# Half of the first tile's output projection summed inside the attention steps of three mixers

## What is computed

```python
def ab_mixer(x, ...):
    ...
    return jnp.concatenate([y_a, y_b], axis=-1) @ w_o

def nsa_mixer(x, ...):
    ...
    return o.reshape(B, S, C_MIX) @ w_o

def _gqa_attention(...):
    ...
    y_lat = jnp.moveaxis(o, 0, 1).reshape(b, n, Q_DIM) @ w_o
```

## Time and profile before

| what | value |
|---|---|
| median of 3 runs | 1934.36 us (1932.5 to 1934.42) |
| the profiled execution, its own time | 1922.37 us |
| its span | 1920.6 us |
| mean granted TensorE clock | 0.92 of full speed |
| PE busy | 1538.6 us (80%) |
| DVE busy | 424.4 us (22%) |
| ACT busy | 248.4 us (13%) |
| moved by DMA | 711.11 MB, mean 370 GB/s |

### The profile page before, as it was taken

The page is one execution under the profiler, slowest core; times in us unless marked ns, Lnnn a source line. Parts: engine busy times, 40 slices in busy tenths (PEclk is TensorE's granted clock), DMA queues, the critical chain, the costliest instruction groups (busy, mean ns, idle before and its releaser), DMA issues.

```text
span 1920.6 us, 23284 instructions
## 1 busy us (share of the span) xinstructions
PE 1538.6 (80%) x10228; PEld 742.0 (39%) x10228; DVE 424.4 (22%) x944; ACT 248.4 (13%) x531; POOL 86.7 (5%) x142
## 2 busy tenths in 40 slices
PE   7898777899898788999977667776799767667676
PEld 4665434664464344444522122221355222122222
DVE  3341110226331112464500000000043000000001
ACT  0310000026312011155100000000011000000000
POOL 1100000101100000112100000000000000000000
PEclk9999899999999999999998888887999888888888
DMA  7559999859879999299599999999987999999996
GB/s 286 216 226 415 423 423 421 313 206 386 338 304 409 420 421 416 92 366 394 224 425 423 424 424 423 423 424 424 420 333 313 423 424 424 423 423 423 424 423 269
DMA packets 128014, 711.11 MB, mean 370 GB/s; under 512 B 8376, under 2 KB 13480, under 8 KB 59296
## 3 DMA queue, kind: packets, MB, share of 16 engines
q1 hardware_dynamic: 121488, 697.14, 88.8%
q0 software_dynamic: 4320, 9.78, 1.5%
q10 hardware_dynamic: 2096, 2.57, 0.4%
HBM read 708.17 MB, written 1.05 MB: 369 GB/s over the span
## 4 chain that ended last, share of the span: by engine, by line
PE 46%; DMA 42%; DVE 5%; SPq 2%; ACT 2%; issue 2%; POOL 1%; DVEq 0%; PEldq 0%; ACTq 0%; POOLq 0%
DMA ring<-in_moe_w 23%; DMA ring<-in_moe_w_down 6%; PE pa L812 6%; PE pb L785 5%; DMA work<-in_moe_w 5%; PE pa L830 4%; PE pb L762 3%; DMA mod<-in_moe_w 3%; PE acc L883 3%; PE acc L1382 3%; PE acc L1387 3%; PE acc L1123 2%; SPq L698 2%; DMA ring<-in_moe_w_up 2%; DMA work<-in_moe_w_down 2%
## 5 line engine op out<-in xcount | busy, mean ns | idle before, releaser
L785 PE MATMUL pb<-ring,XT 128*32 128x512 f32 x1424 | 274.2, 716 | 90.8 <-DMA ring<-in_moe_w 90.5
L812 PE MATMUL pa<-ring,work 128*32 128x512 f32 x928 | 188.2, 742 | 68.8 <-DMA ring<-in_moe_w 44.5
L785 PEld LDWEIGHTS pb<-ring,XT 128*32 128x32 f32 x1424 | 62.3, 127 | 252.8 <-DMA ring<-in_moe_w 131.6
L929 DVE TENSOR_TENSOR work<-work,pb 128x256 f32<-128x256 f32 (+1 forms) x32 | 17.7, 554 | 586.7 <-PE pb L785 438.3
L883 PE MATMUL acc<-XT,work 128*128 128x512 f32 x256 | 118.4, 605 | 35.3 <-DVE XT L939 22.4
L830 PE MATMUL pa<-work,HM 128*128 128x128 f32 x1024 | 128.2, 286 | 16.0 <-issue 16.0
L830 PEld LDWEIGHTS pa<-work,HM 128*128 128x128 f32 x1024 | 126.8, 203 | 30.5 <-issue 30.5
L785 PE MATMUL pb<-work,XT 128*32 128x512 f32 x480 | 111.0, 682 | 27.7 <-DMA work<-in_moe_w 27.7
L762 PE MATMUL pb<-ring,XT 128*32 128x256 f32 x1600 | 113.3, 407 | 16.1 <-DMA ring<-in_moe_w_up 16.1
L812 PEld LDWEIGHTS pa<-ring,work 128*32 128x32 f32 x928 | 42.2, 130 | 179.7 <-issue 78.5
L892 ACT COPY XT<-pa 128x512 f32<-128x512 f32 x32 | 18.8, 586 | 592.2 <-PE pa L830 592.2
(11 more groups left out here) (410 smaller groups left out, 1775.8 us busy)
## 6 DMA issues: line engine op xcount, KB each, us to landing
ring<-in_moe_w SPq DMA_DIRECT2D x135, 2048.0 KB
work<-in_moe_w SPq DMA_DIRECT2D x46, 2048.0 KB
ring<-in_moe_w_up SPq DMA_DIRECT2D x28, 2048.0 KB
ring<-in_moe_w_gate SPq DMA_DIRECT2D x26, 2048.0 KB
ring<-in_moe_w_down SPq DMA_DIRECT2D x24, 2048.0 KB
ring<-in_w_mod SPq DMA_DIRECT2D x48, 1024.0 KB
mod<-in_moe_w SPq DMA_DIRECT2D x11, 2048.0 KB
work<-in_moe_w_down SPq DMA_DIRECT2D x8, 2048.0 KB
```

The costliest lines, as they stand in the source:

```text
L785: last = nc.tensor.matmul(hbank[m][j * CAP:(j + 1) * CAP, :], m_xg[:, k, j * CAP:(j + 1) * CAP], slot_of(s0 + j // 2)[:, at:at + fn], star ...
L812: last = nc.tensor.matmul(pa[j * CAP:(j + 1) * CAP, h, :], m_ht[:, c, j * CAP:(j + 1) * CAP], slot_of(i)[:, at:at + 512], start=(c == 0), ...
```

## The change

A new function `early_out_tensor` does the second half of the columns (512 to 1023) of tile 0 for some of the chunks, and is called at the end of given steps of the attention: in ab chunk 0 in step 1, 1 in step 2, 2 in step 3, 3 and 4 in step 4, 5 in step 5; in nsa chunk 0 in step 13, 1 in 14, 2 and 3 in 15, 4 in 16, 5 and 6 in 17; in gqa chunks 0 and 1 in step 16 and 2 in step 17. `out_tensor` then does the chunks that are left of that half, each as soon as its own heads are copied, and after them the first half of the columns (bank `acc[:, 0, 0:512]`, which the attention uses) once all heads are copied. Each matmul of tile 0 now has a wait for heads and a wait for its slot ahead of it, in all four mixers. In fourier the order of the matmuls and the counts waited for stay. Tile 1 is as it was.

```diff
--- before.py
+++ after.py
@@ -1367,20 +1367,38 @@
                 if sp["extra_vector"]:
                     sp["extra_vector"](dve, i)
 
-        def out_tensor(pe, ph, q0, grouped=False):
+        def heads_ready(ph, t, c):
+
+            if ph.kind == "ab":
+                return ph.out0 + max(1, c - 2)
+            if ph.kind == "nsa":
+                return ph.out0 + c + 1
+            return ph.out0 + (ph.nout // 2 * t + c // 2 + 1 if ph.kind == "gqa" else max(2, c // 2 + 1))
+
+        def out_row(q0, c):
+            return slot(q0 + c // 4).rearrange("p (k c) -> p k c", k=4)[:, c % 4, :]
+
+        def early_out_tensor(pe, ph, q0, chunks):
+
+            for c in chunks:
+                pe.wait_ge(s_out, heads_ready(ph, 0, c))
+                slot_wait(pe, q0 + c // 4)
+                nc.tensor.matmul(acc[:, 0, 512:D], XT[:, c, 0:P], out_row(q0, c)[:, 512:D], start=(c == 0), stop=(c == KC - 1))
+
+        def out_tensor(pe, ph, q0, early=0):
 
             def row(c):
-                return slot(q0 + c // 4).rearrange("p (k c) -> p k c", k=4)[:, c % 4, :]
-
-            pe.wait_ge(s_out, ph.out0 + (2 if grouped else ph.nout))
-            for c in range(KC):
-                if grouped and c in (4, 6):
-                    pe.wait_ge(s_out, ph.out0 + c // 2 + 1)
-                if c % 4 == 0:
-                    slot_wait(pe, q0 + c // 4)
-                for h in range(2):
-                    last = nc.tensor.matmul(acc[:, 0, h * 512:(h + 1) * 512], XT[:, c, 0:P], row(c)[:, h * 512:(h + 1) * 512],
-                                            start=(c == 0), stop=(c == KC - 1))
+                return out_row(q0, c)
+
+            if early:
+                parts = [(1, c) for c in range(early, KC)] + [(0, c) for c in range(KC)]
+            else:
+                parts = [(h, c) for c in range(KC) for h in range(2)]
+            for h, c in parts:
+                pe.wait_ge(s_out, ph.out0 + ph.nout if early and h == 0 else heads_ready(ph, 0, c))
+                slot_wait(pe, q0 + c // 4)
+                last = nc.tensor.matmul(acc[:, 0, h * 512:(h + 1) * 512], XT[:, c, 0:P], row(c)[:, h * 512:(h + 1) * 512],
+                                        start=(c == 0), stop=(c == KC - 1))
             last.then_inc(mix_done, 1)
             for h in range(2):
                 for c in range(KC):
@@ -1527,8 +1545,12 @@
                     for c in range(4):
                         last = nc.tensor.transpose(second_heads(h)[0][:, c, :], HM[:, 1, (4 * h + c) * P:(4 * h + c + 1) * P], ident[:, :])
                     last.then_inc(qt_ps, 1)
+                if i in OUT_AT:
+                    pe.wait_ge(part_copied, 2 * MODC)
+                    early_out_tensor(pe, ph, ph.slot_mod + MODC, OUT_AT[i])
+            OUT_AT = {16: (0, 1), 17: (2,)}
             att_tensor(pe, ph, gqa_spec(extra))
-            out_tensor(pe, ph, ph.slot_mod + MODC)
+            out_tensor(pe, ph, ph.slot_mod + MODC, early=3)
 
         def gqa_scalar(act, ph):
             moe = plan[ph.i - 2]
@@ -1717,7 +1739,7 @@
                             last = nc.tensor.matmul(acc[:, c // 4, (c % 4) * TOK + at_:(c % 4) * TOK + at_ + n], waves(i, s, c % 2),
                                                     f_a[:, 2 * g + i, at_:at_ + n], start=(c % 2 == 0 and s == 0 and i == 0), stop=(i == 1), skip_group_check=True)
                 last.then_inc(f_done, 1)
-            out_tensor(pe, ph, ph.slot0, grouped=True)
+            out_tensor(pe, ph, ph.slot0)
 
         def fourier_scalar(act, ph):
             for g in range(KC // 2):
@@ -1800,7 +1822,7 @@
         TWO_PI = (6.28125, 1.93500518798828125e-3, 3.0198368e-7)
         MAGIC = 1.5 * 2.0 ** 23
 
-        def ab_spec():
+        def ab_spec(extra=None):
             def scores(i, banks):
                 for t in range(TT):
                     for u in range(2):
@@ -1816,7 +1838,7 @@
                         w = TOK - t * P
                         yield (acc[u * MV:(u + 1) * MV, 0, t * P:TOK], b_vals[:, t, (2 * i + u) * MV:(2 * i + u + 1) * MV],
                                weights[:, t * 512 + u * w:t * 512 + (u + 1) * w], t == 0, t == 1)
-            return dict(CAUSAL, scores=scores, values=values, masked=False, gate=None, per_pair=1, extra=None, extra_vector=None, out=lambda n: (XT[:, NGM + n, :], acc[:, 0, 0:TOK]),
+            return dict(CAUSAL, scores=scores, values=values, masked=False, gate=None, per_pair=1, extra=extra, extra_vector=None, out=lambda n: (XT[:, NGM + n, :], acc[:, 0, 0:TOK]),
                         pt=work[:, 4096:6144].rearrange("p (a c) -> p a c", a=2))
 
         def ab_sync(sp, ph):
@@ -1919,8 +1941,12 @@
                 last.then_inc(mla_done, 1)
             pe.wait_ge(b_qktc, 3)
             pe.wait_ge(pad_cleared, 2)
-            att_tensor(pe, ph, ab_spec())
-            out_tensor(pe, ph, ph.slot0 + 4)
+            OUT_AT = {1: (0,), 2: (1,), 3: (2,), 4: (3, 4), 5: (5,)}
+
+            def extra(pe, i):
+                early_out_tensor(pe, ph, ph.slot0 + 4, OUT_AT.get(i, ()))
+            att_tensor(pe, ph, ab_spec(extra))
+            out_tensor(pe, ph, ph.slot0 + 4, early=6)
 
         def ab_scalar(act, ph):
 
@@ -2257,8 +2283,12 @@
             def extra(pe, i):
                 if 1 <= i <= MODC:
                     block_tensor(pe, ph, 0, i - 1, 0)
+                if i == MODC + 1:
+                    pe.wait_ge(part_copied, MODC)
+                early_out_tensor(pe, ph, ph.slot_mod + MODC, OUT_AT.get(i, ()))
+            OUT_AT = {MODC + 1: (0,), MODC + 2: (1,), MODC + 3: (2, 3), MODC + 4: (4,), MODC + 5: (5, 6)}
             att_tensor(pe, ph, nsa_spec(extra))
-            out_tensor(pe, ph, ph.slot_mod + MODC)
+            out_tensor(pe, ph, ph.slot_mod + MODC, early=7)
 
         def nsa_scalar(act, ph):
             transpose_scalar(act, ph.xt, XT)
```

## The result

The change takes 1918.12 us (median of 5 runs, 1917.70 to 1923.11) where the kernel before takes 1932.5 beside it (5 runs, 1925.11 to 1934.42): a ratio of 0.994, 95% interval 0.9915 to 0.9964, or 6.9 to 16.3 us. The forecast, 1927.2 with a range from 1923.0, had the sign and the mechanism, and less than the measured gain. Repeated later, with 11 and 34 runs, the ratio was 0.9947 (0.9929 to 0.9964): 10 us.

What follows compares the result with a forecast made beforehand. PE and DMA in turns were taken to bound the kernel, with mixer gains passed on to the weight streams. Gains of 3.5, 2.9 and 0.75 us, 7.2 in all, off 1934.36 gave 1927.2 us, range 1923.0 to 1933.0.

Steps and rivals of the forecast that it cites:

- What bounds the kernel: Mixers and expert stages: PE and DMA hold 46% and 42% of the chain; all of a mixer's gain is passed on.
- filled up: Rival, mixers and next weight stream: delayed softmax or an unmoved stream leaves 0 to 3.5 us of gain; chance 0.19.
- ab: End of ab's attention: six matmuls moved and a 0.46 us wait gone, less 2.15 us delay, gain 3.5 us.
- nsa: End of nsa's attention: seven matmuls moved, 6.05 us, less 3.15 us delay, gain 2.9 us.
- the price of an inserted matmul: Each early matmul of tile 0 in the attentions' last steps was priced at 0.865 us.
- gqa: End of gqa's attention: three matmuls moved and a 0.47 us wait gone, less 2.3 us delay, gain 0.75 us.
- The waits: Tile 0's matmuls: satisfied waits cost nothing; rival of 12.2 us added by held-back weight loads, chance 0.06.
- The late output matrix: Rival, nsa's first early matmul: output matrix lands late, PE stands from 485, about 11 us lost; chance 0.02.
- The failed step: Final sum: the 12 us between profiled execution and shown median was carried over, 1934.36 less 7.2, giving 1927.2 us.
- More than I count: Rival, expert stages: a different fall of the half-clock spell adds or takes 1 to 2 us each; beyond 11 us, chance 0.03.

Runs made afterwards that it cites:

- between_thrown: Changed kernel, early matmuls between scores and transposes, their sums thrown away and that half redone, against the kernel before: 1925.81 us, ratio 0.9991.
- waits_only: Changed kernel with nothing moved early, only the two waits ahead of every tile 0 matmul, against the kernel before: 1927.79 us, ratio 1.0007.
- ab_only: Changed kernel with early matmuls in ab alone, against the kernel before: 1922.60 us, ratio 0.9976.
- nsa_only: Changed kernel with early matmuls in nsa alone, against the kernel before: 1922.14 us, ratio 0.9974.
- doubled: Changed kernel with early matmuls in place, their sums thrown away and all of that half redone, against the kernel before: 1932.07 us, ratio 1.002.
- between: Changed kernel with 13 early matmuls moved between a step's scores and transposes, against the kernel before: 1912.29 us, ratio 0.9922.
- gqa_only: Changed kernel with early matmuls in gqa alone, against the kernel before: 1928.52 us, ratio 1.0008.
- before_p4: The kernel before, unchanged, one more traced execution: 1935.80 us.
- before_p5: The kernel before, unchanged, another traced execution: 1926.71 us.
- thrown_again1: First repeat, 12 runs, of the version with matmuls between scores and transposes thrown away and redone, against the kernel before: 1925.09 us, ratio 0.9991.
- thrown_again3: Third repeat, 12 runs, of the version with matmuls between scores and transposes thrown away and redone, against the kernel before: 1927.22 us, ratio 0.9999.
- thrown_again2: Second repeat, 12 runs, of the version with matmuls between scores and transposes thrown away and redone, against the kernel before: 1928.18 us, ratio 0.9995.

## Why the prediction was wrong in size

- **What bounds the kernel: right in the main.** The gain of a mixer passes the weight stream. The stream's first load after ab is 4.17 us earlier, as tile 1 is 4.10 earlier (0.6 of it is there at ab's first scores already, and not the change's), and nsa begins 3.7 earlier. The rival "filled up" fell. Not quite all comes through after nsa: from its tile 1 to gqa's scores before takes 311.1 to 313.2 us in seven traces, the changed kernel 312.2 to 313.9 in three, 1.4 more in the mean. As between_thrown and its repeats, which save nothing, take 312.3 to 314.3 there, this need not be gain waited away; why it is longer stays open.
- **ab: right, 3.5 of 3.5.** It was worked out chunk by chunk, with the delay by ACT as the only choice. The hole of 1.85 shows 1.01 left: 0.84 swallowed, as the sum had it.
- **nsa: 2.4 of 2.9 (2.5 in the other three traces with nsa's change).** The term mis-sized is the price of an inserted matmul, which depends on what follows. Ahead of scores it took 1.06 us, not 0.865 (486.54 to 487.60; chunk 0 took 1.05), and the two ahead of the last products took 1.92, not 1.73 (498.07 to 499.99). The scores' delay comes back in the transposes that wait for ACT, as traced, only larger. Another 0.15 of this trace goes with a spell at the attention's start (granted clock 0.87 from 422 to 432 us, 1.00 in the other three).
- **gqa: 0.7 of 0.75.** Right; most of a gain is eaten where the hole is only 0.17.
- **The waits: right at zero.** 115 more waits in waits_only (one less than in the change) give 1.0007, at most 5.4 us by the interval's upper end, and tile 0 takes 13.84 us with them as without. The Trainium skill (Advanced Engine Details and Errata, Network/Comms) prices a sequencer's reading of a semaphore at 50 to 100 ns; the 6 to 12 us estimated from it do not appear where the wait is already satisfied and matmuls follow each other; the page speaks of a reading, not of such a wait. Where that estimate and this run differ, the run decides.
- **The late output matrix: no.** No idle entry stands ahead of 481.48.
- **The failed step: "The median of the runs shown is 12 us above that execution, with nothing in its trace to say why; I take the same difference from the median: 1934.36 - 7.2".** 1934.36 was the median of three executions that all came from the upper part of a scatter of 18 us (1918.9 to 1937.3 beside all experiments); beside the experiments, in the four sets of 17 to 34 runs, the median of before is 1926.3 to 1929.9, so some 4 to 8 us of the 12 belonged to those three executions, not to the kernel. Of the 110 executions in the four sets 20 lie at 1932.5 or above, where all three lay; by chance alone that comes in fewer than one case of a hundred. Whether it was this luck or something about their hour or chip, no run shows. From 1928.1 the same sum gives 1920.9, 2.8 above the result, and the range with it would have held. As a ratio the forecast was 0.9963, just within the intervals (to 0.9964) of both measurements; it is the absolute time that was out of reach. The profiled execution at 1922.4 lay in the lower part of the scatter and the three runs in its upper part; that they disagreed by 12 us was the sign, and I carried it along instead of widening the range downwards for it. The gain beyond the forecast is the smaller part of the miss: of the 9.1 us between 1927.2 and 1918.1, 6.3 are the reference and 2.8 the gain.
- **More than I count: not beyond 11 us, as far as the larger samples tell.** The clock does fall behind the holes that the change fills, in 4 of 10 traces in each of ab and nsa. I had placed this in the expert stages alone. By the 48 runs with the holes filled it is worth 0.5 us, which isn't told from nothing, and not the 3 I first took from the traces.

The account of the 10 us, whose interval is 6.9 to 13.7: 6.6 us by the stretches, which agree in four traces each of ab's and nsa's change; about 0.5 by the filled holes; 3 stay open. Part of these 3 comes of comparing medians: in the means over all executions, 1927.7 us (110 of before) against 1919.0 (17 of the changed kernel), the gain is 8.7 us, by resampling 7.3 to 10.2. The traces don't show the rest: outside the three stretches the seven of before take 1700.3 to 1710.6 us (mean 1703.6), the three of the changed kernel 1704.7 to 1708.5 (mean 1706.2). ab_only, nsa_only, doubled and between each came out 1 to 3.6 us better than their stretches, all within their intervals; but gqa_only came out 2.2 worse, and all but ab_only were measured against one and the same 32 runs of before, whose median, 1929.9, is the highest of the four sets. So it isn't shown that anything is left beyond the stretches.

## What to carry to other kernels

Before taking a difference from a median, ask from how many executions it comes and where the profiled one lies among them: here three runs were off by 6 us, nearly as much as the whole gain. Put filler work where the engine waits for others (between scores and transposes here), not ahead of the work that others wait for: 13 matmuls gained 11.5 us in the stretches there, and 16 gained 6.6 at the steps' ends. Waits that were already satisfied cost nothing that showed beside matmul records that follow each other at 0.43 us.

## What the chip showed that I had not expected

- The kernel before has executions from 1918.9 to 1937.3 us, and the long ones have the lower mean granted clock: before_p4, 1935.8 us at 0.912; before_p5, 1926.7 at 0.918; before, 1922.4 at 0.921. Filling three sets of holes with thrown-away matmuls more than halved this scatter (1922.4 to 1930.4) without moving its middle. Work in gqa's holes alone did so too (1924.7 to 1931.0, 12 runs); why is open.
- A spell at 1.2 GHz costs 1.4 us at the end of ab and up to 5.7 at the end of nsa, where two followed one another; at the start of nsa it costs nothing to 0.4 us (thrown_again1 and 2 against 3). PE has idle time there that takes it up: from 422 to 432 us it is busy 6.51 us in thrown_again3 and 8.28 in thrown_again2.
- An early matmul costs 0.86 us in front of scores whose weights are 128 x 128 (76.20 to 77.06), 1.06 in front of scores whose weights have 64 rows (486.54 to 487.60), and 1.05 in front of products whose weights have 64 columns (91.81 to 92.86).
